# Two-block transformer on one core: the level products of a gated linear recurrence issued with lower and upper partitions in turn

## The reference

```python
def gla_chunked(q, k, v, g, s0, strict):
    ...
    def step(s, inp):
        qc, kc, vc, gc = inp
        b = jnp.cumsum(gc, axis=1)
        o_inter = jnp.einsum('bihk,bhkv->bihv', qc * jnp.exp(b), s)
        decay = jnp.exp(jnp.where(mask, b[:, :, None] - b[:, None, :], -jnp.inf))
        att = jnp.einsum('bihk,bjhk,bijhk->bijh', qc, kc, decay)
        o_intra = jnp.einsum('bijh,bjhv->bihv', att, vc)
        ...
    o_f = gla_chunked(q, k, v, g_f, s_f, False)
    o_b = flip(gla_chunked(flip(q), flip(k), flip(v), flip(g_b), s_b, True))
```

## Time and profile before

| | |
|---|---|
| runs, us | 1523.33, 1528.21, 1517.63; median 1523.33 |
| profiled execution, us | 1517.8, its span 1515.9 |
| TensorE busy, us | 1428.8, in 6938 matmul records |
| VectorE, ScalarE, GpSimd busy, us | 900.3, 399.6, 836.5 |
| TensorE's share of the chain that ended last | 81% |
| DMA queues, mean | 94 GB/s |

### The profile page before, as it was taken

The page is one execution under the profiler, slowest core; times in us unless marked ns, Lnnn a source line. Parts: engine busy times, 40 slices in busy tenths (PEclk is TensorE's granted clock), DMA queues, the critical chain, the costliest instruction groups (busy, mean ns, idle before and its releaser), DMA issues.

```text
span 1515.9 us, 19663 instructions
## 1 busy us (share of the span) xinstructions
PE 1428.8 (94%) x6938; PEld 1160.8 (77%) x6938; DVE 900.3 (59%) x1256; ACT 399.6 (26%) x747; POOL 836.5 (55%) x651
## 2 busy tenths in 40 slices
PE   6899888999879999999999999799799999999998
PEld 4577667888748888888887888588688888888887
DVE  4569778774466666661008688644674888887000
ACT  2350222332242222221002302255422332332000
POOL 0133333332647666667775677333256777777765
PEclk9899899998989999999999999899899999999999
DMA  9537512110203333333332232111122333333332
GB/s 319 158 120 248 160 42 56 56 56 29 84 28 88 100 94 96 96 92 100 92 103 70 84 97 85 55 56 43 42 70 84 97 97 97 97 97 90 101 90 80
DMA packets 224314, 142.04 MB, mean 94 GB/s; under 512 B 5595, under 2 KB 210944, under 8 KB 224256
## 3 DMA queue, kind: packets, MB, share of 16 engines
q1 hardware_dynamic: 222389, 140.11, 31.1%
q10 hardware_dynamic: 1867, 1.12, 0.3%
HBM read 139.12 MB, written 2.10 MB: 93 GB/s over the span
## 4 chain that ended last, share of the span: by engine, by line
PE 81%; DVE 12%; ACT 2%; issue 2%; DMA 2%; POOL 1%; SPq 0%; ACTq 0%; DVEq 0%; POOLq 0%
PE ps L514 24%; PE ps L516 23%; PE ps L515 23%; PE ps L767 2%; DVE ada_acc L1635 2%; PE ps L1037 2%; PE ps L554 2%; DVE norm_acc L1567 1%; PE ps L1007 1%; PE ps L1023 1%; PE ps L595 1%; DMA par_rows<-in_conv_w 1%; DVE xT L1986 1%; DVE SS L1818 1%; DVE g_z L1736 1%
## 5 line engine op out<-in xcount | busy, mean ns | idle before, releaser
L477 POOL TENSOR_TENSOR w_lo<-raw,w_hi 128x1024 fp32r<-128x1024 f32 x213 | 534.7, 2510 | 17.7
L514 PE MATMUL ps<-h_hi,w_hi 128*128 128x512 f32 x1064 | 428.2, 402 | 15.9 <-DVE h_lo L1589 10.0
L515 PE MATMUL ps<-h_lo,w_hi 128*128 128x512 f32 x1064 | 419.5, 394 | 0.0
L516 PE MATMUL ps<-h_hi,w_lo 128*128 128x512 f32 x1064 | 419.3, 394 | 0.0
L473 POOL TENSOR_TENSOR w_hi<-raw,cst 128x16 fp32r<-128x16 f32 x213 | 64.5, 303 | 631.4 <-PE ps L516 567.0
L514 PEld LDWEIGHTS ps<-h_hi,w_hi 128*128 128x128 f32 x1064 | 202.8, 191 | 64.6 <-issue 17.0
L516 PEld LDWEIGHTS ps<-h_hi,w_lo 128*128 128x128 f32 x1064 | 203.0, 191 | 43.9
L515 PEld LDWEIGHTS ps<-h_lo,w_hi 128*128 128x128 f32 x1064 | 203.5, 191 | 39.9
L474 POOL TENSOR_SCALAR w_hi<-raw 128x1008 fp32r<-128x1008 f32 x213 | 231.4, 1086 | 0.0
L1907 DVE SCALAR_TENSOR_TENSOR f_acc<-ps,par,f_acc 128x441 f32<-128x441 f32 (+2 forms) x176 | 122.3, 695 | 48.9 <-ACT f_acc L1105 25.1
L514 PE MATMUL ps<-f_hi,w_hi 128*128 128x512 f32 x352 | 138.4, 393 | 0.2 <-POOL w_lo L477 0.2
(11 more groups left out here) (283 smaller groups left out, 2032.2 us busy)
## 6 DMA issues: line engine op xcount, KB each, us to landing
raw<-in_w_up SPq DMA_DIRECT2D x88, 512.0 KB, 3.9
raw<-in_w_in SPq DMA_DIRECT2D x59, 512.0 KB, 4.0
raw<-in_w_down SPq DMA_DIRECT2D x32, 512.0 KB, 3.8
v_tok<-in_w_ada SPq DMA_DIRECT2D x18, 512.0 KB, 5.7
ada_first<-in_w_ada SPq DMA_DIRECT2D x8, 1024.0 KB, 11.7
raw<-in_w_out SPq DMA_DIRECT2D x16, 512.0 KB, 3.7
ada<-in_w_ada SPq DMA_DIRECT2D x14, 512.0 KB, 6.1
raw<-in_w_down SPq DMA_DIRECT2D x16, 384.0 KB, 3.4
```

Of the source, the lines that this page charges most:

```text
L477: pool.tensor_tensor(w_lo[:, slot % 2, :], raw[:, slot, :], w_hi[:, slot % 2, :].bitcast(F32), ALU.subtract).then_inc(S("lo_split"), 1)
L514: nc.tensor.matmul(dst, lhs_hi, rhs_hi, start=first, stop=False)
L515: nc.tensor.matmul(dst, lhs_hi, rhs_lo, start=False, stop=False)
L516: return nc.tensor.matmul(dst, lhs_lo, rhs_hi, start=False, stop=last)
```

## The change

The two loops of `level` change places. Before, the four heads of the lower partitions came first and then the four of the upper ones; now each head's lower product is followed by its upper one. Operands, banks, waits and the semaphore on the last matmul (head 3, upper) stay.

```diff
             else:
                 pe.wait_ge(S("state_read"), ALL_CHUNKS)
-            for bank, at, half_at in ((4, 0, 1), (5, DK, 0)):
-                for h in range(GH):
+            for h in range(GH):
+                for bank, at, half_at in ((4, 0, 1), (5, DK, 0)):
                     zh = z[at:at + DK, h, :]
                     rhs = zh.rearrange("p (b s t) -> p b s t", s=2, t=half)[:, :, half_at, :]
                     mm = nc.tensor.matmul(ps[:, bank, h * 64:(h + 1) * 64], zh, rhs, start=True, stop=True)
```

## The result

| | before | in turn |
|---|---|---|
| median beside each other, us (6 runs each) | 1523.48 | 1508.19 |
| range of these runs, us | 1517.63 to 1528.21 | 1504.41 to 1514.99 |
| profiled execution and its span, us | 1517.8, 1515.9 | 1514.69, 1512.7 |
| start of the first to start of the last level burst, us | 158.73 | 149.05 |
| one burst, us | 1.60 | 1.11 |

The ratio is 0.9916, with a 95% interval from 0.9891 to 0.9942: 8.8 to 16.6 us less. The forecast of 1513.3 us was 10.0 less than 1523.3; the measured median is 5 us under it and inside the range of 1506.5 to 1520.5.

What follows compares the result with a forecast made beforehand. TensorE, busy 1428.8 of 1515.9 us, was taken as the bound. Twenty bursts at 0.48 and two at 0.8 give 11.2 us, less 1.1 at VectorE's waits, rounded to 10: 1523.3 to 1513.3 us, range 1506.5 to 1520.5.

Steps and rivals of the forecast that it cites:

- The price of a burst: Level burst at L767: sixteen passes in 1.12 us instead of 1.60, priced from L1007 and L657; 0.48 us saved each.
- the rivals that left the burst at 1.60 us or made it longer: L767 bursts: pairs don't form, time 1523 (chance 0.08); or alternation serialises, 1533, at worst 1583 (0.05).
- The estimate by the sequencer's 62 ns: L767 burst by the skill's page: 1.20 us, 0.40 saved each, 8.8 us in all; set aside for the trace's rows.
- the signs that the prediction named: Bursts 1.1 us, seven or eight passes mid-burst, L767 some 25 us, burst of 368.0 near 358, fourth-level gaps awaiting g_att.
- The step that was mis-sized: Chunks 1 and 2: VectorE's work, hanging on TensorE's head sum after burst 263.56, moves up with earlier bursts, not 268.84's.
- The loss per chunk: Chunks 1 and 2: VectorE's late takes cost 0.56 us each, so 1.1 us come off 11.2.
- ahead of the fourth level: Chunk 1, burst at 274.21 behind VectorE's take: room for 0.09 us, so 0.39 of 0.48 lost; chunk 2 repeats it.
- ahead of the fifth (0.17): Chunk 1, burst at 278.69: VectorE needs 4.17 us between takes, TensorE 4.00 plus 0.15; another 0.17 lost; chunk 2 repeats it.
- The clock: Rival: more TensorE idling brings new 0.50-clock stretches, 2.7 us each; two leave 5 us of gain, 1518 (chance 0.10).
- more arrives: Rival: the six off-chain bursts count too, 14 us, plus a slow stretch gone, 2.7: 1506 us (chance 0.05).

Runs made afterwards that it cites:

- the trace with the take first: Changed kernel with VectorE's take of the last level ahead of the offsets of the level after next; ratio to before 0.9927.
- moving the reciprocal: Changed kernel with the reciprocal of head factors (L1792) behind VectorE's fourth-level products instead of ahead; ratio to before 0.9890, four runs.
- other orders on VectorE's queue: Changed kernel with take earlier, reciprocal later, or both plus second-level products ahead of L1774, states' advance later or kept; ratios 0.9927, 0.9890, 0.9919, 0.9905 and 0.9916.
- two and two: Changed kernel's level loop reordered to two lower products, two upper, two lower, two upper; ratio to before 0.9926, median 1509.96 us.
- three and one: Changed kernel's level loop reordered to three lower products, three upper, then the fourth lower and upper; one run, 1517.62 us.
- off the chain only: Kernel before, in turn only at the six levels not in its chain (steps 0, 2, 3, 4, 21, 22 of 28); ratio 0.9987.
- before with take first: Kernel before (by halves) with VectorE's take moved ahead of the offsets; ratio 0.9991.

## Why the prediction was right

**The price of a burst** was 1.12 us, bounds 1.09 and 1.16; measured 1.11. L774 against L1007 told it, and the rivals that left the burst at 1.60 us or made it longer (a switch of halves costs time) have nothing for them: 1.11 us at full clock, 1.22 behind the diagonal. The passes follow one another by (1.11 - 0.27)/15 = 0.056 us. The estimate by the sequencer's 62 ns (the Trainium skill, "TensorE: Matmul & The Clock Gate", section "Wait - 56ns, not 53.3ns?") would have been 1.20 us for a burst; the trace doesn't bear it out here.

**The sum by chunks.** The stretches of the traces against the working ahead of the runs:

| | before | after | saved | forecast |
|---|---|---|---|---|
| chunk 0 | 49.81 | 47.92 | 1.9 | 1.8 |
| chunk 1 | 38.45 | 36.05 | 2.4 | 2.8 |
| chunk 2 | 38.45 | 36.05 | 2.4 | 2.8 |
| start of the 22nd to start of the 28th level | 32.01 | 29.02 | 3.0 | 2.2 |
| start of the first to start of the 28th | 158.73 | 149.05 | 9.7 | 9.6 |

(The forecast's part: chunk 0 two fast bursts and one slow, chunks 1 and 2 seven of 0.48 less 0.56, the last stretch one slow and three; the 28th burst, whose 0.48 us makes it 10.1, lies behind its own start.) From the first burst to the end the two profiled executions took 1306.6 and 1296.6 us, 10.0 apart. That this is the very number of the forecast is in part luck: one term was too small and another too large, as told next, and the other three traces of the changed kernel took 1293.5, 1294.4 and 1293.5 us, 12 to 13 less than before; chunk 0 alone saved 3.8, 2.1 and 3.8 us in them. Of the signs that the prediction named, the last burst starts at 365.19 and not near 358 only because this execution reached its recurrence 6.87 us later.

**The step that was mis-sized** is "VectorE's work up to there hangs on a head sum of TensorE ... so it moves up with the earlier bursts". It hung on ScalarE, which reached its table load no sooner (8.96 us into the chunk against 8.94), and on the reciprocal that waits for it at the head of VectorE's queue. The loss per chunk was 1.03 us in place of 0.56. Against the trace with the take first, 0.74 of it is lost ahead of the fourth level, where 0.39 was forecast, 0.18 ahead of the fifth (0.17), and 0.1 ahead of the second, which the forecast didn't have. The direction and the name of the wait were as forecast; moving the reciprocal gave 0.58 of it back, moving the take all of it. My working took one row, the matmul nearest in time, for the releaser, though the idle time ahead of the reciprocal is put down to ScalarE.

The last stretch made up for it, with 0.8 us over its forecast. The clock is at 0.50 for 10.2 us there in both. Before, that ended at 352.0, 6.9 us after the start of the 24th burst (345.07); after, at 350.0, 4.8 us behind it (345.25). So 2.1 us less of TensorE's dense work ran at 1.2 GHz. This is not a term I had. It is no draw of one execution either: that time is 4.7 to 5.4 us in the four traces of the changed kernel and 6.7 to 7.5 in the three kernels whose bursts on the chain go by halves. Why is open; with other orders on VectorE's queue it was 4.5 to 6.5, two and two 5.2, three and one 6.8.

**The clock** didn't give the gain back. The mean of the profiled executions is 0.961 in the first trace of the changed kernel and 0.961 to 0.966 in all four, against 0.965. From 254.5 to 339.8 us it stayed at full clock in spite of the new waits. Stretches at 0.50 moved: in the first trace after, two of 3.4 us in chunk 0 replaced one of 6.8.

```profile
237.40:240.80 3.40, 3.40 (x15) 2.73 (x13) 3.32 (x11) 0.00 (x0) 0.00 (x0) 0.50 0.26 78
251.10:254.50 3.40, 3.40 (x9) 2.75 (x9) 3.34 (x9) 0.89 (x2) 0.00 (x0) 0.50 0.00 0
339.80:350.00 10.20, 8.52 (x47) 7.65 (x48) 8.23 (x18) 6.91 (x12) 0.00 (x0) 0.50 0.15 50
254.50:339.80 85.30, 81.20 (x573) 67.43 (x572) 65.56 (x106) 29.99 (x56) 38.44 (x30) 1.00 0.20 57
```

**Why the median fell by more than 10.** All 27 runs of the changed kernel have a mean of 1508.2 us, and 75 of before 1521.3: 13.1 us less, give or take 2. The recurrence holds 9.7 to 11.4 of them by the four traces of the changed kernel against the one of before, and its last burst 0.5. A smaller part lies behind it, in the stretch between the norms. Counting from the last pass of the last burst, a place some 400 matmul records on comes 109.5 us later in the three traces whose on-chain bursts go by halves (before, off the chain only, before with take first), and 108.4 to 108.7 in the eleven others. There the clock stood at 0.50 for 10.2 us in the former and 6.8 in the latter (stretches of before, then of after):

```profile
410.10:420.30 10.20, 6.71 (x14) 3.21 (x13) 7.04 (x11) 3.12 (x5) 5.91 (x4) 0.50 0.18 51
```

```profile
408.10:414.90 6.80, 3.91 (x5) 1.76 (x6) 5.90 (x9) 1.99 (x5) 3.51 (x3) 0.50 0.26 77
```

That is 1.1 us more, at a place with none of the change's instructions. Why the clock comes back sooner there is open, and no run tells whether an earlier arrival does it. Nor do the traces show whether more of the clock is in the 13.1 us. Over all runs its mean rose, 0.9638 in the 27 of the changed kernel against 0.9606 in the 69 of before beside the experiments. In those 69, 0.001 of clock goes with 1.3 us, an estimate by which the difference would be 4 us, part of it perhaps within the recurrence. The profiled run of before, at 0.965 and 1517.8 us, was one of its faster ones and hides this. Of the rivals, "more arrives" had a grain of truth, by this; that the bursts off the chain add to it is not shown.

## What to carry to other kernels

Here products on 64 partitions left the other half of the array idle for part of the time unless that half's products came within two fp32 matmuls in the order (always into another PSUM bank; no run tried the same one). Reordering them adds no work and took 0.49 us from 1.60. Look for a second place in the trace that already issues in turn, it gives the price. Then ask for each saved stretch which instruction of the next engine stands right behind it and what that one really waits for: nearly a third of the gain in chunks 1 and 2 went to a reciprocal and a take that had cost nothing before.

## What the runs showed of the hardware

**How far ahead the other half is found.** Four orders of the same eight matmuls gave 1.11, 1.13 to 1.16, 1.38 and 1.60 us. They fit one distance, four passes (two fp32 matmuls with their weight loads), at either clock, and I had not expected so sharp a limit.

**Matmuls on different halves leave the program's order.** In the timeline of after above, a pass of the level starts at 287.50, and a pass of the diagonal product, which stands ahead of it in the order, at 287.61. The Trainium skill, "TensorE: Matmul & The Clock Gate", section "The mechanism", says that matmuls start and end in program order, without reordering; of the starts the measurement shows otherwise.

**GpSimd's pass at L477 holds back VectorE's work that reads two inputs from SBUF**, not its copies out of PSUM. Products of 0.75 us took 2.27 us, offsets of 0.69 took 2.42, and eight advances, 1.16 for four elsewhere, took 5.29. The two copies of the take at 284.58 in the trace of after lie inside such a pass (284.20 to 286.91) and took 0.42 and 0.43 us, as outside one. The pass starts after TensorE has freed a slot, so TensorE's pace decides which of VectorE's instructions meets it; with the reciprocal later, VectorE's own order did too.
